# Decoder step on one core: when value pages and state copies are issued, and how eight sample tokens are projected and spread

## What is computed

```python
h = normalize(x) * (1 + scale1) + shift1
qa, ka, va, qb, kb, vb, ga, gb = split(h @ w_in)       # 1024 x 5888
oa = block-sparse attention, 8 heads of 64 (sample: 2048 cached keys/values in 16 pages of 128)
ob = dilated windows, strides 1, 4, 16 x 4 heads (sample: 128 kept rows of a state buffer)
mix = (sigmoid(ga) * (oa @ w_proj_a) + sigmoid(gb) * (ob @ w_proj_b)) @ w_out
x = LN1(alpha * x + gate1 * mix)
h = normalize(x) * (1 + scale2) + shift2
y = sum over the top 2 of 32 experts: w * ((silu(h @ w_eg[e]) * (h @ w_eu[e])) @ w_ed[e])
x = LN2(alpha * x + gate2 * y)
new state buffers: the old ones moved on by one row, with the new key and value at the end
```

## Time and profile before

| | |
|---|---|
| median of the runs | 1111.47 us (1106.67 to 1111.61) |
| the profiled execution | 1108.21 us, span in the profile 1106.1 us |
| busy | PE 852.6 us (77%), DVE 344.9 (31%), ACT 182.7 (17%), POOL 116.2 (11%) |
| mean granted TensorE clock | 0.893 |
| DMA | 396.30 MB, mean 358 GB/s |
| by queue | SP (q1) 294.97 MB, POOL (q0) 85.90 MB, ACT (q10) 14.93 MB |
| chain that ended last | PE 44%, DMA 37%, DVE 12%, issue 3%, ACT 2% |

### The profile page before, as it was taken

How to read it: one execution, slowest core, us unless ns; L and a number is a source line. 1 busy time by engine, 2 the same in 40 slices (tenths; PEclk the granted TensorE clock), 3 DMA queues, 4 the chain that set the end, 5 groups by cost and what they waited for, 6 DMA issues and landing times.

```text
span 1106.1 us, 11674 instructions
## 1 busy us (share of the span) xinstructions
PE 852.6 (77%) x4564; PEld 466.1 (42%) x4564; DVE 344.9 (31%) x520; ACT 182.7 (17%) x429; POOL 116.2 (11%) x116
## 2 busy tenths in 40 slices
PE   6599898988989999992507877878777878777840
PEld 5484675467764445872504322323222322222310
DVE  2048997883143321327501000000000000000008
ACT  2311223232121210003302111111111110111110
POOL 1212211121001112000010000000000000000020
PEclk9799999999898885996657999999999999999985
DMA  9976999889889999959983999999999999999931
GB/s 317 399 299 262 401 408 408 310 321 409 287 296 379 429 394 339 371 223 341 326 315 134 426 424 426 427 426 424 426 425 425 427 426 425 425 424 424 424 119 43
DMA packets 70452, 396.30 MB, mean 358 GB/s; under 512 B 6530, under 2 KB 15254, under 8 KB 47959
## 3 DMA queue, kind: packets, MB, share of 16 engines
q1 hardware_dynamic: 49728, 294.97, 67.3%
q0 software_dynamic: 12016, 85.90, 19.5%
q10 hardware_dynamic: 8672, 14.93, 3.8%
HBM read 387.89 MB, written 58.10 MB: 403 GB/s over the span
## 4 chain that ended last, share of the span: by engine, by line
PE 44%; DMA 37%; DVE 12%; issue 3%; ACT 2%; SPq 1%; POOL 0%; ACTq 0%; POOLq 0%; DVEq 0%
DMA ring<-in_w_exp_up_dram 27%; PE bank L800 12%; PE bank L435 8%; DMA ring<-in_w_in_dram 5%; PE bank L632 3%; DVE ring L1216 3%; DVE S L1220 3%; PE bank L445 3%; PE bank L715 3%; DMA listed_tokens<-v,didx 2%; PE bank L702 1%; PE bank L461 1%; PE bank L487 1%; DMA ring<-in_cache_k_pages_dram,pidx 1%; PE bank L818 1%
## 5 line engine op out<-in xcount | busy, mean ns | idle before, releaser
L800 PE MATMUL bank<-ring,hT 128*64 128x512 f32 x1024 | 241.8, 627 | 43.3 <-DMA ring<-in_w_exp_up_dram 40.8
L800 PEld LDWEIGHTS bank<-ring,hT 128*64 128x64 f32 x1024 | 88.9, 143 | 194.9 <-issue 194.9
L435 PE MATMUL bank<-hT,ring 128*128 128x264 f32 x576 | 140.6, 402 | 10.6 <-DMA ring<-in_w_in_dram 10.6
L1597 DVE TENSOR_TENSOR hT<-hT,bank 128x256 f32<-128x256 f32 x32 | 19.2, 601 | 415.0 <-ACT hT L1140 415.0
L818 PE MATMUL bank<-ring,hT 128*64 128x512 f32 x512 | 120.3, 611 | 19.5 <-DVE hT L1600 19.5
L435 PEld LDWEIGHTS bank<-hT,ring 128*128 128x128 f32 x576 | 111.7, 198 | 32.4 <-DMA ring<-in_w_in_dram 7.8
L1216 DVE TENSOR_TENSOR ring<-ring,qbc 128x4096 f32<-128x4096 f32 x16 | 70.8, 4422 | 42.7 <-ACTq L845 40.9
L1737 POOL DMA_INDIRECT expert_rows<-work,ridx x32 | 31.1, 971 | 477.9 <-ACT work L837 355.6
L818 PEld LDWEIGHTS bank<-ring,hT 128*64 128x64 f32 x512 | 41.4, 139 | 77.8 <-issue 77.8
L837 ACT ACTIVATE work<-bank 128x512 f32<-128x512 f32 (+5 forms) x83 | 36.7, 451 | 223.8 <-PE bank L818 145.9
L1220 DVE TENSOR_REDUCE S<-ring 128x64 f32<-128x4096 f32 x16 | 70.6, 4415 | 0.3
(11 more groups left out here) (303 smaller groups left out, 785.8 us busy)
## 6 DMA issues: line engine op xcount, KB each, us to landing
ring<-in_w_exp_up_dram SPq DMA_DIRECT2D x32, 2048.0 KB, 22.0
ring<-in_w_exp_down_dram SPq DMA_DIRECT2D x32, 2048.0 KB, 21.6
ring<-in_w_exp_gate_dram SPq DMA_DIRECT2D x32, 2048.0 KB, 17.4
ring<-in_w_ada_dram SPq DMA_DIRECT2D x12, 2048.0 KB, 15.2
ring<-in_w_in_dram SPq DMA_DIRECT2D x11, 2048.0 KB, 22.8
out_dram<-in_state_dil_kv_dram SPq DMA_DIRECT2D x5, 4064.0 KB
out_dram<-in_state_dil_kv_dram ACTq DMA_DIRECT2D x24, 508.0 KB, 8.7
out_dram<-in_state_dil_kv_dram SPq DMA_DIRECT2D x8, 992.0 KB
```

Source lines behind the costliest of these rows:

```text
L435: i = mm(bk[:, 0:NT], w[:, k, j * P:(j + 1) * P], hT3[:, k, :], start=(k == 0), stop=(k == KC - 1))
L800: i = mm(side(2, half).rearrange("p (m n) -> p m n", m=2), xT[s][:, k, :], w[:, :, k, half * 256:(half + 1) * 256], start=(k == 0), stop=( ...
```

## The change

Six things, in the order of the program:

- Queries of the samples are turned once into rows (`query_rows`): for tile 0 four products, for tile 4 six, 8 rows out of each, which ACT copies to `qrow`, unused rows 32 to 39 of `v`. A spread is then one product of 512 columns (or 256 for `spread_b`) with 8 rows of the identity, one of them repeated, as the stationary matrix.
- `win_v8` makes the values of the 8 sample tokens in four column tiles of 32 that share a bank, 32 products of 128 (for tile 7: 64) columns instead of 8 of 512 (256). ACT empties the four parts by four copies.
- `EARLY` falls from 3 to 2, and the pieces on ACT's queue begin at tile 7, not 5: 16 pieces, not 24.
- The first two value halves wait until the last tile of `w_in` has landed.
- SP's copies are spread over the waits for the six expert slots: 2 of 4 MB, then 2 after two loads, then 2 of 4 MB and 2 of 1 MB after two more; behind the last load stand six of 1 MB, eight of 0.2 MB and `copy_rest`. Those six and eight are cut in runs of at most 4096 bytes, not 16384.
- The listed rows are loaded back on ACT's queue, not on SP's.

```diff
-EARLY = 3
+LATE_RUN = 4096
+EARLY = 2
@@ PE
-            def spread(row, b):
-                return zT3[:, row, SEQ + b:SEQ + b + 1].to_broadcast([P, P])
+            def win_v8(w, c0, n):
+                bk = take(("v", c0, 2), acc[0] % 2)
+                acc[0] += 1
+                m = n // 4
+                for k in range(KC):
+                    for j in range(4):
+                        i = mm(bk[32 * j:32 * j + NB, 0:m], hT3[:, k, SEQ:NT], w[:, k, j * m:(j + 1) * m],
+                               start=(k == 0), stop=(k == KC - 1))
+                done(("v", c0, 2), i)
+                return i
+            def query_rows(kind, r0, rn, c0):
+                for h in range(0, rn, 4):
+                    bk = take(("qr", kind, h), 2 + h // 4)
+                    for j in range(min(4, rn - h)):
+                        i = mm(bk[32:32 + NB, j * P:(j + 1) * P], zT3[:, r0 + h + j, SEQ:NT], ident, start=True, stop=True)
+                    done(("qr", kind, h), i)
+            def spread(b):
+                return ident[32:32 + NB, 32 + b:33 + b].to_broadcast([NB, P])
@@ PE, spread_b
+                pe.wait_ge(s_qrow, 3)
...
-                        for c in range(2):
-                            o = b % 2 * 256 + c * P
-                            i = mm(bk[:, o:o + P], spread(ZROW[QB] + 2 * g + c, b), ident, start=True, stop=True)
+                        i = mm(bk[:, b % 2 * 256:b % 2 * 256 + 256], spread(b),
+                               qrow[:, AW + g * 256:AW + (g + 1) * 256], start=True, stop=True)
@@ PE, loop over the tiles
-                        i = win_v(w, *V_TILES[t], tt)
+                        i = win_v(w, *V_TILES[t], tt) if tt < 2 else win_v8(w, *V_TILES[t])
...
+                if t == 0:
+                    pe.wait_ge(s_z, 4)
+                    query_rows("a", ZROW[QA], 4, 0)
+                    pe.wait_ge(s_qrow, 1)
                 for b in Q_AFTER.get(t, ()):
-                    pe.wait_ge(s_z, 4)
                     bk = take(("qbc", b), 2 + b % 2)
-                    for j in range(4):
-                        i = mm(bk[:, j * P:(j + 1) * P], spread(ZROW[QA] + j, b), ident, start=True, stop=True)
+                    i = mm(bk[:, :], spread(b), qrow[:, 0:AW], start=True, stop=True)
                     done(("qbc", b), i)
+                if t == 4:
+                    pe.wait_ge(s_z, 14)
+                    query_rows("b", ZROW[QB], 6, AW)
@@ ACT, loop over the tiles
-                        if t >= 5:
+                        if t >= 7:
                             copy_piece()
@@ ACT, behind the router
+            act.wait_ge(s_xsd, 6 * 16)
+            for t, (r0, rn) in enumerate(XT):
+                act.dma_start(xrow[t][0:rn, :], xs_d[r0:r0 + rn, :]).then_inc(s_xrow[(0, 1, 1, 2, 2)[t]], 16)
@@ POOL
             for hh in range(2):
                 pool.wait_ge(s_kred, 2 * NB - 1 + hh)
+                if hh == 0:
+                    pool.wait_ge(w_full[slot_of(("win", 11))], ring_use["win", 11][2])
                 page_half(v_pages, 0, hh, VSLOT[hh], v_full[hh])
@@ SP
+            late = [(2, b) for b in range(EARLY, NB)] + [(g, b) for g in (1, 0) for b in range(NB)]
             for at, slot in enumerate((4, 5, 0, 1, 2, 3)):
-                if at == 0:
-                    copy_state(2, EARLY)
-                    copy_state(2, EARLY + 1)
+                if at % 2 == 0:
+                    for g, b in (late[0:2], late[2:4], late[4:NB - EARLY + 2])[at // 2]:
+                        copy_state(g, b, COPY_RUN)
                 filled(sp, ...)
                 load_expert(slot // 3, slot % 3, slot // 3)
-            for b in range(EARLY + 2, NB):
-                copy_state(2, b)
-            for g in (1, 0):
-                for b in range(NB):
-                    copy_state(g, b)
+            for g, b in late[NB - EARLY + 2:]:
+                copy_state(g, b, LATE_RUN)
             for g in range(NG):
                 copy_rest(g)
-            sp.wait_ge(s_xsd, 6 * 16)
-            for t, (r0, rn) in enumerate(XT):
-                sp.dma_start(xrow[t][0:rn, :], xs_d[r0:r0 + rn, :]).then_inc(s_xrow[(0, 1, 1, 2, 2)[t]], 16)
```

26 lines of the change are left out of this document (21 added, 5 removed).

## The result

The changed kernel takes 1103.6 us (median of 16 runs, 1100.39 to 1108.35), the one before 1110.42 us beside it (16 runs): ratio 0.9943, 95% interval 0.9930 to 0.9956. The forecast was 1088 us, 21.0 us faster by its sum, with 1081 to 1101 as its range: the direction held, a third of the size came. The profiled execution of the changed kernel took 1103.56 us, with a span of 1101.5 us against 1106.1 before.

What follows compares the result with a forecast made beforehand. It took DMA as the limit for value pages and expert weights, PE and DVE for the projection. Terms summing to -21.0 us from 1108.2 gave 1087.2, with half the distance to the median 1088 us; range 1081 to 1101.

Steps and rivals of the forecast that it cites:

- Query rows: Front, tile 0: turning the queries once into rows and spreading by one product each adds 1.2 us.
- `spread_b`: Front: five groups of query spreads with eight products of 256 columns instead of 16 instructions save 1.0 us.
- Values of 8 tokens: Front, tiles 5 to 7: cheaper 8 token products on PE shorten DVE's waits, saving 3.9 us.
- Hold: End of the projection: holding back two value halves lets the late w_in tile land in time, saving 6.9 us.
- Value stage: After the projection: the held value halves still arrive before they are used up, costing nothing, with 3 us of cover.
- Scatter: Last scatter of token rows, from 551 us: short copy runs give it about half the DMA bandwidth, saving 14.4 us.
- Listed rows: Loading the rows back after the scatter: on ACT's queue they share the DMA engines with remaining copies, adding 4.0 us.
- SP's queue: Before the expert loop: copies end at 584 us, before the router's chain at 592, costing nothing, with 8 us cover.
- the case "slower": Rival: copies ahead of the expert loads push the queue's end past the loop's first load; 1116 us, chance 0.05.
- The sign that I had named for a failure of the whole: Start of the expert loop: the forecast fails as a whole if the first load is not issued before 595 us.
- ACT's first DMA: Rival, front: the 5.64 us issue belongs to ACT's first DMA, putting 5.3 us onto the path; 1094 us, chance 0.20.
- "No change": Rival: held value halves come late by the front's 10.6 us and the scatter is not relieved; 1109.5 us, chance 0.10.

Runs made afterwards that it cites:

- e5: The changed kernel with the copies that stood behind the last expert load (8.6 MB) moved behind the expert loop's last weight load; 1103.1 us, ratio 0.9937.
- e7: The changed kernel with the last copies in runs of at most 16384 bytes instead of 4096; 1110.3 us, ratio 1.0001.
- e9: The changed kernel with only three 1 MB copies ahead of the scatter, the other 5.5 MB waiting until the listed rows have landed; 1098.6 us, ratio 0.9879.
- e2: The changed kernel with the old spreading of the queries, without query rows and their copies; 1102.3 us, ratio 0.9926.
- e6: The same kernel as e2 (changed kernel, old spreading of the queries), run again; 1097.4 us, one run.
- e10: e9 with the old spreading of the queries; 1092.0 us, ratio 0.9828 of the kernel before.
- e3: The changed kernel with six products of unused content added on PE after turning tile 0's queries, before the wait for their copy; 1109.6 us, ratio 0.9978.
- e12: The changed kernel with the values of the 8 tokens made as in the kernel before; 1106.9 us, ratio 0.9954.
- e11: e10 with the values of the 8 tokens made as in the kernel before; 1086.6 us, ratio 0.9778 of the kernel before.
- e1: The kernel before with only the hold added: the first two value halves wait for the last tile of w_in; 1108.2 us, ratio 0.9970.
- e18: The changed kernel with filler products on PE after turning tile 0's queries and ahead of the 8 token values in tiles 2, 6, 7; 1104.5 us, one run.

## Why the prediction was wrong, point by point

- **Query rows, +1.2 us: the step that failed most.** They cost 6.8 us at the end of the projection (by the means of the table of fronts; 326.4 to 329.2 us in the changed kernel, e5 and e7 to e9, against 318.8 to 321.2 in e2, e6 and e10). The terms I listed, 0.8, 1.0 and 1.9 against 2.05 less 0.1, make 1.55 and not 1.2; measured were 1.04, 0.77 and 2.00 us, and at the first score it was 3.9 us. I left out that PE's granted clock falls behind the wait for ACT's copy: 1.7 us in tile 1 (e3 shows the cause, and that filling the wait gives back 0.9 net). I left out the six products at tile 4 altogether (1.1 us of PE, 1.4 on the path). A spread by one product took what four products took, 1.12 us against 1.05 to 1.16, so nothing came back. The slow block at 156 us is no part of this: e2, e6 and e10, without query rows, have it too (5.9 to 6.0 us).
- **`spread_b`, -1.0 us: nothing.** 1.99 us a group, against 1.95 to 2.05 before.
- **Values of 8 tokens, -3.9 us: right beside the query rows, nothing without them.** The price on PE was right (1.93 us). What it is worth depends on the rest, since the waits of DVE move. With the query rows the change gains 3.7 us in front (263.76 us in e12, a single run, 260.02 with the new values). With the old spread no gain is shown there (253.24 us on average, 251.76 with the old values, in ranges that overlap), and the time is better without it (e11 against e10). Both changes on PE together cost 8.3 us in front (260.02 less 251.76); -3.7 was forecast for them, `spread_b` taken in.
- **Hold, -6.9 us: right,** 9.0 alone and 7.4 in the changed kernel. What the query rows cost in front used it up.
- **Value stage, nothing: missed by a little.** In the changed kernel it waits 3.0 us for pages; in e1 3 us of the 9 are gone by the scatter. It can take more: in e2, e5, e9, e12 and e18 PE waits for one of the last pages and then stands 4.0 to 4.5 us with no releaser in the profile, where all other runs have 0.3 to 1.6 us. What PE waits for there stays open.
- **Scatter, -14.4 us: 11.7 in size, and right in mechanism but for the turns.** The length of the runs counts, as e7 shows: 7.6 of the 11.7 us. The other 4.1 came without it. I had the packets alternate one to one and the scatter take half of the engines; it got one packet in three and a third of the bytes, and landed at 570.1 us, not by 566. By my own terms 28 us less 11 would have been 17, not 14.4.
- **Listed rows, +4.0 us: right,** +3.9.
- **SP's queue, nothing: right,** from 580 to 598 us the DMA share is 0.00, so no copy was left when the loop's first load went out. But the working was not: it set the queue's end, 584 us, against 592, while the forecast itself needs the load at 582, 2 us before that end.
- **From the first products of the loop to its first load, nothing: +1.7 us,** 1.2 of it slower products (9.95 us at a granted clock of 0.71, against 8.74 at 0.83).
- **Two sums beside.** The forecast's own bounds make 1080 to 1096 us, not 1081 to 1095. And if the end is the first load plus 503 us, the case "slower" begins with the queue's end at 603 us, not 619, and 625 us makes about 1130 us, not 1116.

The sum of the forecast's front was -10.6 and came out as -0.2 us; behind it -10.4 was foreseen, and -4.4 is what the table of the result gives from the projection to the end. The sign that I had named for a failure of the whole came: the loop's first load was issued at 598.17 us, not before 595. Of the rivals none was it: ACT's first DMA took 0.40 us, the scatter was sped up, the load of `w_in` came in time. "No change" had the front's gain given back by the value stage, and that is the nearest, by another mechanism: the query rows spent the gain before it reached that stage. What stays open: where the query rows lose the 1.5 us that remain of the 6.8 besides the 3.9 up to the first score and the 1.4 at tile 4; why the time of e11 is better than e10's; why e3's time was worse than the changed kernel's; and why SP's queue sent two packets for one of POOL's.
